# One expert slot in four taken from TensorE's diagonal products to a multiply and sum on VectorE

## The reference, cut to what matters

```python
gate = jax.nn.softmax(sc, axis=-1)
act = jax.nn.gelu(jnp.einsum('thkd,td->thk', u_tab[e], xb), approximate=False)
return jnp.einsum('thk,thkd->td', gate * act, v_tab[e])
```

## Time and profile before

| what | value |
|---|---|
| runs, median (lowest, highest) | 2923.81 us (2922.86, 2925.49) |
| profiled execution, its own time | 2928.07 us |
| its span | 2926.4 us |
| busy: TensorE, VectorE, ScalarE, GpSimd | 2565.0, 1525.8, 906.5, 799.4 us |
| moved by the DMA | 937.70 MB, of it 694.73 MB by GpSimd's queue |
| mean granted TensorE clock | 0.963 |

### The profile page before, as it was taken

One profiled execution on the slowest core, in us unless ns is written; L12 is line 12 of the kernel. 1 busy time (PEld: TensorE's weight loads), 2 busy tenths in 40 slices (PEclk: granted clock), 3 DMA queues, 4 the chain that ended last, 5 costly groups with the idle time before them and its releaser, 6 DMA issues.

```text
span 2926.4 us, 26223 instructions
## 1 busy us (share of the span) xinstructions
PE 2565.0 (88%) x8280; PEld 1324.8 (45%) x8280; DVE 1525.8 (52%) x3674; ACT 906.5 (31%) x2428; POOL 799.4 (27%) x705
## 2 busy tenths in 40 slices
PE   7999999899967879989988899799899988888876
PEld 3555555444323644445544355444455443443332
DVE  1330022111011875569865678755698657666674
ACT  2110111000021443255532454432545334343332
POOL 0011100000000233344333333333443324444453
PEclk8999999999978999999999999999999999999999
DMA  5133324444346699999999999999999999999996
GB/s 213 49 111 110 118 84 159 176 159 168 115 156 229 268 425 426 427 418 411 377 426 427 426 416 360 425 426 426 420 408 380 426 427 426 412 427 426 424 418 290
DMA packets 138038, 937.70 MB, mean 320 GB/s; under 512 B 16503, under 2 KB 20855, under 8 KB 35241
## 3 DMA queue, kind: packets, MB, share of 16 engines
q0 software_dynamic: 98720, 694.73, 57.0%
q1 hardware_dynamic: 33562, 200.40, 17.9%
q10 hardware_dynamic: 5616, 40.90, 3.4%
HBM read 898.16 MB, written 37.81 MB: 320 GB/s over the span
## 4 chain that ended last, share of the span: by engine, by line
DMA 28%; PE 24%; DVE 8%; ACT 4%; DVEq 2%; issue 2%; POOL 1%; ACTq 0%; SPq 0%; POOLq 0%
DMA e_expert<-in_peer_uv,e_idx 27%; PE e_acc L1548 15%; DVE e_expert L1666 3%; PE e_qs L1563 3%; PE e_B L1481 2%; DVEq L1668 1%; ACT e_diag L1434 1%; POOL e_expert L1345 1%; PE e_A L1481 1%; ACT e_coef L1429 1%; PE e_A L849 0%; DMA e_wb<-in_w_out 0%; ACT e_act L1426 0%; ACT e_mg L909 0%; ACTq L1430 0%
## 5 line engine op out<-in xcount | busy, mean ns | idle before, releaser
L1548 PE MATMUL e_acc<-e_expert,e_diag 128*128 128x512 f32 x2560 | 1206.1, 618 | 236.0 <-ACT e_diag L1434 235.6
L1345 POOL DMA_INDIRECT e_expert<-in_peer_uv,e_idx x640 | 757.2, 1183 | 1294.0 <-PE e_acc L1548 1110.7
L1666 DVE CUSTOM_DVE_ANT_0 e_expert<-e_expert,e_xb 128x1024 f32<-128x1024 f32 x640 | 777.1, 1224 | 495.1 <-DMA e_expert<-in_peer_uv,e_idx 466.3
L1548 PEld LDWEIGHTS e_acc<-e_expert,e_diag 128*128 128x128 f32 x2560 | 484.2, 197 | 872.2 <-issue 515.4
L514 PE MATMUL pj<-w_chunk,hT 128*128 128x512 f32 x800 | 357.5, 605 | 9.5 <-DMA w_chunk<-in_w_big 7.3
L1426 ACT ACTIVATE e_act<-e_dots 128x2 f32<-128x2 f32 x320 | 65.0, 203 | 850.9 <-DVEq L1668 849.4
L514 PEld LDWEIGHTS pj<-w_chunk,hT 128*128 128x128 f32 x800 | 154.0, 195 | 196.4 <-issue 193.4
L1434 ACT ACTIVATE e_diag<-ident,e_coef 128x128 f32<-128x128 f32 x640 | 221.9, 394 | 22.3 <-issue 0.4
L484 PE MATMUL pj<-hT,w_chunk 128*128 128x512 f32 x512 | 226.4, 595 | 0.0
L1429 ACT ACTIVATE e_coef<-e_act,e_gate 128x1 f32<-128x1 f32 x640 | 154.0, 287 | 23.0 <-issue 1.1
L1563 PEld LDWEIGHTS e_qs<-e_h2T,e_w_head 128*128 128x128 f32 x1280 | 148.0, 192 | 9.8 <-issue 9.6
(11 more groups left out here) (369 smaller groups left out, 2139.2 us busy)
## 6 DMA issues: line engine op xcount, KB each, us to landing
e_wb<-in_w_out SPq DMA_DIRECT2D x60, 1024.0 KB
e_w_head<-in_w_q ACTq DMA_DIRECT2D x39, 1024.0 KB
w_chunk<-in_w_big SPq DMA_DIRECT2D x18, 2048.0 KB, 9.0
w_chunk<-in_w_mod SPq DMA_DIRECT2D x8, 2048.0 KB, 9.1
scratch_proj<-tile_out POOLq DMA_DIRECT2D x10, 1280.0 KB
e_expert<-in_peer_uv,e_idx POOLq DMA_INDIRECT x640
wm<-in_w_mod SPq DMA_DIRECT2D x4, 2048.0 KB, 20.5
e_m<-scratch_mod_rows SPq DMA_DIRECT2D x15, 512.0 KB, 7.5
```

Of the source, the lines that this page charges most:

```text
L1345: nc.gpsimd.indirect_dma_start(expert[:, u % RING, :], None, dr["peer_uv"], bass.IndirectOffsetOnAxis(idx[:, h % 4, s:s + 1], 0)).then_inc ...
L1548: mm = nc.tensor.matmul(acc[:, c * 512:(c + 1) * 512], diag[:, (u + j) % RING, :], expert[:, (u + j) % RING, D + c * 512:D + (c + 1) * 512 ...
L1666: nc.vector.tensor_tensor_reduce(expert[:, u % RING, 0:D], expert[:, u % RING, 0:D], xb[p % 2][:, :], 1.0, 0.0, ALU.mult, ALU.add, dots[:, ...
```

## The change

One slot in four (`u % 4 == 3`) is summed on VectorE, but in the first head of a block, where `f` still holds the block before. For such a slot ScalarE builds no diagonal and TensorE does no product. VectorE takes the slot's `v` half, multiplies it by the weight in `coef` and adds it to `f` in SBUF (`vector_products`; the first such slot of a block writes `f` by a multiply alone). It does so one pair later: in each body the dots of the pair come first, then the vector products of the pair before. GpSimd waits for such a slot on a semaphore of its own, `vector_free`. `coef` becomes a ring of four pairs. At the block's end `block_sum` moves from ScalarE to VectorE, after the vector products, and adds `acc` to `f`.

```diff
@@ -1147,7 +1147,14 @@
 SCAN_STEPS = 29
 MERGE_FROM, MERGE_TO = 21, 62
 PIECE_AT = (34, 35, 37, 39, 41, 42, 44, 46, 48, 49, 51, 53)
+ON_VECTOR = [u // TOPK % HP != 0 and u % 4 == 3 for u in range(HEADS * TOPK)]
 PIECES = ((0, 0, 0), (0, 0, 1), (1, 0, 0), (1, 0, 1), (0, 1, 0), (0, 1, 1), (1, 1, 0), (1, 1, 1), (2, 0, 0), (2, 1, 0), (2, 0, 1), (2, 1, 1))
+
+
+def earlier(u):
+
+    same = [v for v in range(u) if ON_VECTOR[v] == ON_VECTOR[u]]
+    return len(same)
 
 
 def experts(nc, dr, t):
@@ -1169,7 +1176,7 @@
         hot, number = sb("hot", [P, 2, TOPK, TOPK]), sb("number", [P, 2, TOPK])
         arg, expo, total = sb("arg", [P, TOPK]), sb("expo", [P, TOPK]), sb("total", [P, 2])
         idx, gate = sb("idx", [P, 4, TOPK], U32), sb("gate", [P, 4, TOPK])
-        dots, act_v, coef = sb("dots", [P, 2, TOPK]), sb("act", [P, 2]), sb("coef", [P, 2])
+        dots, act_v, coef = sb("dots", [P, 2, TOPK]), sb("act", [P, 2]), sb("coef", [P, 4, 2])
         diag, zero = sb("diag", [P, RING, P]), sb("zero", [P, P])
         ss, root, rr = sb("ss", [P, 1]), sb("root", [P, 1]), sb("rr", [P, 1])
 
@@ -1202,7 +1209,7 @@
         h2_turned, h2T_half, q_mm, q_moved, s_mm, S_moved, scored = (
             sem("h2_turned"), sem("h2T_half"), sem("q_mm"), sem("q_moved"), sem("s_mm"), sem("S_moved"), sem("scored"))
         arg_ready, exp_ready, chosen = sem("arg_ready"), sem("exp_ready"), sem("chosen")
-        in_slot, slot_free = [sem(f"in_slot{j}") for j in range(RING)], sem("slot_free")
+        in_slot, slot_free, vector_free = [sem(f"in_slot{j}") for j in range(RING)], sem("slot_free"), sem("vector_free")
         dots_ready, diag_ready = sem("dots_ready"), sem("diag_ready")
         f_mm, acc_free, ss_ready, ms_ready, root_ready, y_ready, y_out, x1_in, row_in = (
             sem("f_mm"), sem("acc_free"), sem("ss_ready"), sem("ms_ready"), sem("root_ready"), sem("y_ready"), sem("y_out"),
@@ -1341,7 +1348,7 @@
                 if s == 0:
                     pool.wait_ge(chosen, h + 1)
                 if u >= RING:
-                    pool.wait_ge(slot_free, u - RING + 1)
+                    pool.wait_ge(vector_free if ON_VECTOR[u - RING] else slot_free, earlier(u - RING) + 1)
                 nc.gpsimd.indirect_dma_start(expert[:, u % RING, :], None, dr["peer_uv"],
                                              bass.IndirectOffsetOnAxis(idx[:, h % 4, s:s + 1], 0)).then_inc(in_slot[u % RING], 16)
 
@@ -1404,12 +1411,6 @@
                 act.wait_ge(h2_turned, 2 * p + part + 1)
                 nc.scalar.copy(flat(h2T[:, 4 * part:4 * part + 4, :]), qs[:, :]).then_inc(h2T_half, 1)
 
-            def block_sum(p):
-                act.wait_ge(f_mm, p + 1)
-                if p:
-                    act.wait_ge(y_ready, p)
-                nc.scalar.copy(f[:, :], acc[:, :]).then_inc(acc_free, 1)
-
             def squares(p):
                 act.wait_ge(acc_free, p + 1)
                 nc.scalar.activation(sq[:, :], f[:, :], ACT.Square, accum_out=ss[:, :])
@@ -1426,20 +1427,23 @@
                 nc.scalar.activation(act_v[:, :], dots[:, m % 2, 2 * n:2 * n + 2], ACT.Gelu)
                 act.drain()
                 for j in range(2):
-                    nc.scalar.mul(coef[:, j:j + 1], act_v[:, j:j + 1], gate[:, m % 4, 2 * n + j:2 * n + j + 1])
+                    nc.scalar.mul(coef[:, n % 4, j:j + 1], act_v[:, j:j + 1], gate[:, m % 4, 2 * n + j:2 * n + j + 1])
                 act.drain()
-                if u >= RING:
-                    act.wait_ge(slot_free, u - RING + 2)
-                for j in range(2):
-                    last = nc.scalar.mul(diag[:, (u + j) % RING, :], t["ident"][:, :], coef[:, j:j + 1])
-                last.then_inc(diag_ready, 1)
+                on_pe = [v for v in (u, u + 1) if not ON_VECTOR[v]]
+                used = [v - RING for v in on_pe if v >= RING and not ON_VECTOR[v - RING]]
+                if used:
+                    act.wait_ge(slot_free, earlier(used[-1]) + 1)
+                for v in on_pe:
+                    last = nc.scalar.mul(diag[:, v % RING, :], t["ident"][:, :], coef[:, n % 4, v - u:v - u + 1])
+                if on_pe:
+                    last.then_inc(diag_ready, 1)
+                else:
+                    act.sem_inc(diag_ready, 1)
 
             def body(m, n):
                 c = m + 2
                 if m and m % HP == 0:
-                    if n == 0:
-                        block_sum(m // HP - 1)
-                    elif n == 1:
+                    if n == 1:
                         squares(m // HP - 1)
                     elif n == 4:
                         block_root(m // HP - 1)
@@ -1460,7 +1464,6 @@
                     run(m, n)
 
             def finish():
-                block_sum(BLOCKS - 1)
                 squares(BLOCKS - 1)
                 block_root(BLOCKS - 1)
 
@@ -1543,10 +1546,12 @@
             def products(m, n):
                 u = m * TOPK + 2 * n
                 pe.wait_ge(diag_ready, m * GROUPS + n + 1)
-                for j in range(2):
+                for v in (u, u + 1):
+                    if ON_VECTOR[v]:
+                        continue
                     for c in range(2):
-                        mm = nc.tensor.matmul(acc[:, c * 512:(c + 1) * 512], diag[:, (u + j) % RING, :],
-                                              expert[:, (u + j) % RING, D + c * 512:D + (c + 1) * 512], start=False, stop=False)
+                        mm = nc.tensor.matmul(acc[:, c * 512:(c + 1) * 512], diag[:, v % RING, :],
+                                              expert[:, v % RING, D + c * 512:D + (c + 1) * 512], start=False, stop=False)
                     mm.then_inc(slot_free, 1)
 
             def body(m, n):
@@ -1668,6 +1673,24 @@
                 dve.drain()
                 dve.sem_inc(dots_ready, 1)
 
+            def vector_products(m, n):
+                u = m * TOPK + 2 * n
+                mine = [v for v in (u, u + 1) if ON_VECTOR[v]]
+                if mine:
+                    dve.wait_ge(diag_ready, m * GROUPS + n + 1)
+                for v in mine:
+                    by = coef[:, n % 4, v - u:v - u + 1]
+                    value = expert[:, v % RING, D:2 * D]
+                    if not any(ON_VECTOR[v - v % SLOTS:v]):
+                        nc.vector.tensor_scalar(f[:, :], value, by, None, ALU.mult).then_inc(vector_free, 1)
+                    else:
+                        nc.vector.scalar_tensor_tensor(f[:, :], value, by, f[:, :], ALU.mult, ALU.add).then_inc(vector_free, 1)
+                    dve.drain()
+
+            def block_sum(p):
+                dve.wait_ge(f_mm, p + 1)
+                nc.vector.tensor_tensor(f[:, :], acc[:, :], f[:, :], ALU.add).then_inc(acc_free, 1)
+
             def choose(c, n):
                 two = range(2)
                 if n == 2:
@@ -1752,8 +1775,12 @@
                 c = m + 2
                 if m >= 0:
                     dot_pair(m, n)
+                if m * GROUPS + n > 0:
+                    vector_products(m - (n == 0), (n - 1) % GROUPS)
                 if m and m % HP == 0:
-                    if n == 3:
+                    if n == 0:
+                        block_sum(m // HP - 1)
+                    elif n == 3:
                         block_mean(m // HP - 1)
                     elif n == 6:
                         block_result(m // HP - 1)
@@ -1766,6 +1793,8 @@
                     choose(c, n - 2)
 
             def finish():
+                vector_products(HEADS - 1, GROUPS - 1)
+                block_sum(BLOCKS - 1)
                 block_mean(BLOCKS - 1)
                 block_result(BLOCKS - 1)
 
```

## The result

The changed kernel takes **2949.17 us** (median of 4 runs, 2943.66 to 2951.60) against 2923.34 (4 runs, 2922.29 to 2925.49): ratio **1.0086**, 95% interval 1.0074 to 1.0098, so 21.6 to 28.6 us slower. The prediction said 2938, range 2917 to 2960.

The account below looks back on a forecast made before the run. VectorE was taken to bound the dense stretches, the DMA-fed ring the rest. 21.6 us left there, less 6.3 caught up and 1.5 at the end, made +13.8 on 2923.81: 2938 us, range 2917 to 2960.

Parts of the forecast that it names:

- The bound: Expert stage: VectorE's work sets the length of the dense stretches; elsewhere the ring turns as fast as the DMA fills it.
- dense stretches: 1320-1438, 1721-1841, 2123-2241 us, where the next block's scan shares VectorE: 32.4 us added, 10.8 hidden in waits, 21.6 remain.
- The product: VectorE's multiply-add for a moved slot, 128x1024: about 1.28 us, counted as 1.37 to the next instruction's start.
- catching up: Right behind the dense stretches, gathers landing ahead shorten VectorE's 12.6 us of waits; half is credited, 6.3 us.
- the removal on TensorE: Expert stage: 140 slots taken off TensorE, 238 us of its work, costed at nothing but for the end.
- the signs: If right: dense stretches 5 to 10 us longer each, VectorE's gather waits near nothing, DMA below 383 GB/s there.
- The light stretches: Rest of the expert stage: 119 products, 163 us, covered by 455 us of VectorE's waits; as long as before.
- The issue beside two inputs from SBUF: GpSimd's gather issues lengthen on a port shared with VectorE: about 34 us for 140 products, costed at nothing.
- Slower still: Rival, 0.13: longer gather issues reach the path, 2972 us, or a quarter of light-stretch products isn't evened out, 2979.
- 238 us less: Sign if right, over the whole kernel: TensorE is busy some 238 us less.
- The end: After the last dot: four passes replace eight, -1.70 us, the addition replaces the copy, +0.2; together -1.5 us.

Follow-up runs that it names:

- run 3: The change, but TensorE keeps all products; VectorE does 140 multiply-adds on tile `xb`, overwritten by a copy at the block's sum: 2953.18 us, 1.0100.
- run 12: The changed kernel with the scan's dt multiplies on VectorE folded into ScalarE's exponential bias, nothing moved in memory: 2927.84 us, 1.0012.
- run 11: The kernel before with the scan's dt multiplies on VectorE folded into ScalarE's exponential bias, nothing moved in memory: 2921.06 us, 0.9989.
- run 5: The change, with TensorE multiplying zeros for each moved slot, as many passes as before: 2952.27 us, 1.0094.
- run 1: The change, but the 21 moved slots of the dense stretches stay on TensorE, 119 still move: 2930.57 us, 1.0015.
- run 2: The change, but only the 21 slots of the dense stretches move, the other 119 stay on TensorE: 2939.75 us, 1.0047.
- run 4: The change's later slot release, but no products on VectorE; TensorE keeps all products and the block's sum is a VectorE copy: 2928.88 us, 1.0019.
- run 7: The kernel before with `block_sum` alone on VectorE, as a copy, and the longer `coef`; no slot moves: 2924.24 us, 0.9997.
- run 6: The change, with vector products over 512 of 1024 columns, the other half of the moved slots left out: 2938.78 us, 1.0046.
- run 10: The changed kernel with the scan's dt multiplies folded into the exponential bias through a new list, later tiles 640 bytes further on: 2951.29 us, 1.0093.
- run 9: The kernel before with the scan's dt multiplies folded into the exponential bias through a new list, later tiles 640 bytes further on: 2942.53 us, 1.0062.

## Why the prediction was right

**The bound.** As read: in the dense stretches VectorE (run 3: its time alone makes the whole loss; run 12: with other work taken off it the change ends 3 us above before, 7 above run 11), elsewhere the DMA. The reading was right for an addition only: by run 11 VectorE was not the one bound of these stretches, since less work on it did not shorten them. The figure that invites the change is TensorE's 88% of busy matmuls; relieving it lost 0.86%. The Trainium skill, "Perfetto Trace Analysis", Identifying the Most-Contended Engine, warns of that figure: it judges TensorE by useful work and by the share of its weight loads, which is 45% on the page of before, below VectorE's 52%. The runs agree. In Optimization Strategy, the section after it, the Trainium skill says that the most-contended engine can change over time, and the windows agree too: VectorE waits 0.6 us for gathers in 75.7 here, 297 over the span.

**The product.** 1.285 us against 1.28 from the nearest row, and 1.38 from its start to the next instruction's (1399.96 to 1401.34) against 1.37. In the timeline of a block's end in after (start, us, line) the dot, the product and the addition follow each other without a wait, as forecast:

```profile
1398.61 1.22 DVE L1671 CUSTOM_DVE_ANT_0 e_expert<-e_expert,e_xb 128x1024 f32<-128x1024 f32 x1
...
1399.96 1.29 DVE L1687 SCALAR_TENSOR_TENSOR e_f<-e_expert,e_coef,e_f 128x1024 f32<-128x1024 f32 x1
1401.34 1.22 DVE L1692 TENSOR_TENSOR e_f<-e_acc,e_f 128x1024 f32<-128x1024 f32 x1
```

**The dense stretches.** 21.6 us were priced before any catching up; first and second part grew by 22.0 - 0.3 = 21.7. The agreement is partly luck. The first part alone was six products three times, 18 x 1.37 = 24.7 less its waits, 1.3 + 1.6 + 1.3 = 4.2, that is 20.5, and grew by 22.0. The second had two terms that met: run 5 shows it 5.3 us longer than before with TensorE loaded, and the relief takes that back. I had costed the removal on TensorE at nothing; there it is worth 5 to 6 us. By the cut of the earlier trace rows, both parts together, the three stretches are 8.2, 5.7 and 7.8 us longer and the DMA moves 364 to 369 GB/s, as the signs had it.

**The catching up.** This is the term that was mis-sized. Half of 12.6 us was credited, 6.3; the rest of the stage gave back 1.1 (1539.5 to 1538.4; 1539.2 and 1539.3 in runs 3 and 5). I had named why it would be little (the DMA is full behind the dense stretch), and took the middle all the same. Without the credit the working gives 2944; the other 5 us are taken up under what stays open.

**The light stretches.** Covered, as said: 423 to 426 GB/s in after, and the rest 1.1 us shorter with 119 products more. Run 1, which has only these, took 1543.3 there, run 2, which has none of them, 1535.5; all runs that move nothing in memory lie between, so some 4 us either way can't be told from one profile.

**The issue beside two inputs from SBUF.** The mean over 640 issues fell from 1183 to 1156 ns where the rule would have it rise. That alone settles little, since run 4, with no such product, has 1156 too: the mean moves with the order of the lists as well. With TensorE's list as before, run 3 has 1196 with the 140 products and run 7 1180 without: some 10 us over all issues, where the prediction's rate gave 34. GpSimd waits 948 us for TensorE's slots in after, and in run 3 dense and the head behind hold the whole loss. Costing it at nothing held, and "Slower still" had no part in it.

**TensorE.** 238 us less were named as a sign, 138 came: the passes grew from 618 to 675 ns, while the mean granted clock fell from 0.963 to 0.922. It costs no time (run 5). **The end** is 1.72 shorter at the products and 0.22 longer at the sum, as priced.

**What stays open.** By the profiles the loss is 18.8 us, by the medians 25.8. Before's own profiled execution lies 4.3 us above its median (the prediction's sum), and its first dot at 994.9 us. In the profiles of the seven experiments in which TensorE's list is as long as before, the first dot comes at 988.1 to 991.7; in the five where it is much shorter (after and runs 1, 6, 10, 12) at 994.9 to 998.8, and in run 2 at 993.9. The instructions ahead of it are those of before or nearly. So some 4 to 6 us of the median's loss, and perhaps as much of run 1's 5.2, may be lost ahead of the expert stage; with one profile a kernel, and before's own at 994.9, this is not shown. The wait that differs most there is TensorE's for the weights, here of after and of run 7:

```profile
PE pj L514 <- DMA w_chunk<-in_w_big: 9.8, 4, 3.7
```

```profile
PE pj L514 <- DMA w_chunk<-in_w_big: 6.2, 3, 3.1
```

It is 9.8 in runs 1 and 12 too, and 6.1 to 6.7 in 3, 5 and 11; before has 7.3. That is 2.5 to 4 us of it; what makes a later part of the program change an earlier one, no run here shows.

## What to carry to other kernels

Look for the stretch in which an engine waits for nothing, whatever its share of the whole span: work added there is paid in full, and what another engine is relieved of is not seen there. Credit a stretch behind it with catching up only if the transfers there have room; with the DMA full it gives back next to nothing. At a kernel that is balanced between two bounds, price a cut by the waits that would open and an addition by the waits that would close, which are not the same.

## What the hardware showed that I had not expected

Moving the tiles of the expert stage by 640 bytes in each partition cost some 20 us (runs 9 and 10 against 11 and 12: the rest is 1560 and 1561 against 1540): the DMA, at the same full share, moved 415 to 421 GB/s in place of 423 to 427 in four windows of the light stretches. Why it does so no run here shows. A comparison of two kernels whose buffers lie at different places can differ by 0.7% for that alone. In the change itself the ring `expert` keeps its place, and run 7 has what lies behind `coef` where the change has it.
